# A four-layer fp32 transformer stack on one core: head-norm sums by token block on 128 partitions, inverse roots updated in PSUM, high and low scales spread by one product

## What is computed

```python
def rms_norm(x, g):
    xf = x.astype(jnp.float32)
    y = xf * lax.rsqrt(jnp.mean(xf * xf, axis=-1, keepdims=True) + EPS)
    return (y * g.astype(jnp.float32)).astype(x.dtype)

# in the attentions, per head:
q = rms_norm(q.reshape(B, S, HEADS, HEAD_DIM), q_gain)
k = rms_norm(k.reshape(B, S, KV_HEADS, HEAD_DIM), k_gain)
```

## Time and profile before

| | |
|---|---|
| median of 3 runs | 2533.02 us (2532.95 to 2538.74) |
| the profiled execution | 2532.64 us, of which the profile's span is 2530.8 us |
| mean granted TensorE clock | 0.972 of full |
| PE busy | 2378.3 us, 94% of the span |
| POOL busy | 1685.3 us, 67% |
| DVE busy | 1113.7 us, 44% |
| ACT busy | 495.5 us, 20% |
| HBM | 82 GB/s mean |

### The profile page before, as it was taken

How to read it: one execution, slowest core, us unless ns; L and a number is a source line. 1 busy time by engine, 2 the same in 40 slices (tenths; PEclk the granted TensorE clock), 3 DMA queues, 4 the chain that set the end, 5 groups by cost and what they waited for, 6 DMA issues and landing times.

```text
span 2530.8 us, 29132 instructions
## 1 busy us (share of the span) xinstructions
PE 2378.3 (94%) x10786; PEld 1915.5 (76%) x10786; DVE 1113.7 (44%) x1306; ACT 495.5 (20%) x926; POOL 1685.3 (67%) x1370
## 2 busy tenths in 40 slices
PE   5978999999997899999999799999999898999999
PEld 4766788888766678888887568888877675888887
DVE  7674543322367444332248645215344443550440
ACT  3245111110124511111011511001111163110000
POOL 5465677777746567777776668767775554776774
PEclk9988999999998899999999899999999999999999
DMA  4300122222320012222232122222222200222222
GB/s 143 113 17 17 61 89 99 99 83 93 114 98 24 17 67 85 98 99 85 92 122 100 39 79 83 100 100 100 98 102 84 84 17 17 95 95 96 97 100 83
DMA packets 37840, 207.88 MB, mean 82 GB/s; under 512 B 3532, under 2 KB 10316, under 8 KB 16888
## 3 DMA queue, kind: packets, MB, share of 16 engines
q1 hardware_dynamic: 37752, 206.70, 23.5%
HBM read 204.55 MB, written 2.13 MB: 82 GB/s over the span
## 4 chain that ended last, share of the span: by engine, by line
PE 59%; DVE 4%; POOL 2%; ACT 2%; issue 1%; DVEq 0%; POOLq 0%; ACTq 0%
PE ps L822 18%; PE ps L827 18%; PE ps L826 18%; POOL wl L650 1%; PE ps L1184 1%; PE ps L895 1%; PE ps L1158 1%; ACT rt L1334 1%; DVE nt L1702 0%; DVE t L1710 0%; DVE nt L1710 0%; POOL wh L644 0%; POOL act L722 0%; PE ps L1159 0%; PE ps L1160 0%
## 5 line engine op out<-in xcount | busy, mean ns | idle before, releaser
L650 POOL TENSOR_TENSOR wl<-raw,wh 128x512 fp32r<-128x512 f32 (+1 forms) x776 | 1049.3, 1384 | 0.0
L644 POOL TENSOR_SCALAR wh<-raw 128x1024 fp32r<-128x1024 f32 (+1 forms) x388 | 430.7, 1130 | 597.1 <-PE ps L822 469.9
L822 PE MATMUL ps<-h,wh 128*128 128x512 f32 x1576 | 617.3, 392 | 21.8 <-POOL wl L650 9.2
L827 PE MATMUL ps<-h,wl 128*128 128x512 f32 x1576 | 613.9, 390 | 0.0
L826 PE MATMUL ps<-h,wh 128*128 128x512 f32 x1576 | 613.8, 389 | 0.0
L822 PE MATMUL ps<-act,wh 128*128 128x512 f32 x1120 | 437.9, 391 | 3.1 <-POOL act L722 2.1
L826 PE MATMUL ps<-act,wh 128*128 128x512 f32 x1120 | 436.3, 390 | 0.0
L827 PE MATMUL ps<-act,wl 128*128 128x512 f32 x1120 | 436.2, 389 | 0.0
L822 PEld LDWEIGHTS ps<-h,wh 128*128 128x128 f32 x1576 | 296.2, 188 | 91.3 <-issue 26.3
L826 PEld LDWEIGHTS ps<-h,wh 128*128 128x128 f32 x1576 | 296.2, 188 | 62.0 <-issue 1.0
L827 PEld LDWEIGHTS ps<-h,wl 128*128 128x128 f32 x1576 | 296.1, 188 | 61.8
(11 more groups left out here) (339 smaller groups left out, 2824.9 us busy)
## 6 DMA issues: line engine op xcount, KB each, us to landing
raw<-w_gu SPq DMA_DIRECT2D x44, 1024.0 KB, 4.8
raw<-w_up SPq DMA_DIRECT2D x32, 1024.0 KB, 4.8
raw<-w_down_b SPq DMA_DIRECT2D x32, 1024.0 KB, 4.9
raw<-w_down_a SPq DMA_DIRECT2D x32, 704.0 KB, 4.0
raw<-w_in_a SPq DMA_DIRECT2D x14, 1024.0 KB, 4.9
raw<-w_in_f SPq DMA_DIRECT2D x13, 1024.0 KB, 4.9
raw<-w_in_r SPq DMA_DIRECT2D x11, 1024.0 KB, 4.9
raw<-w_out_a SPq DMA_DIRECT2D x8, 1024.0 KB, 7.7
```

Of the source, the lines that this page charges most:

```text
L644: pool.tensor_scalar(hi_s[:, part], raw[s][:, part], 1.0, 1.0, ALU.mult, ALU.mult).then_inc(hi_done, 1)
L650: ins = pool.tensor_tensor(lo_s[:, part], raw[s][:, part], hi_s[:, part].bitcast(F32), ALU.subtract)
L822: first = pe.matmul(out, w_hi, v_hi, start=start, stop=False)
L827: return pe.matmul(out, w_lo, v_hi, start=False, stop=stop)
```

## The change

1. `gathered`: the product over 512 (or 256) tokens becomes four of 128 (or 64) tokens each; block q goes to the partitions 32q to 32q+31 of the same bank. The sums of 16 groups by 512 tokens stand on 128 partitions by 128 columns instead of 32 by 512.
2. ACT's `stat` does one more instruction, Square of the first root, into `nt[:, 2]`. Head norms run on 128 x 128 (128 x 64).
3. DVE's Newton step keeps its running value in the PSUM bank: for head norms three instructions (scalar_tensor_tensor, tensor_scalar, tensor_tensor), for row norms four, each with at most one input in SBUF. The bank is handed back (`free[b]`) after the last of them instead of after the first.
4. `head_stat` then writes the high part (four tensor_scalar of 32 x 128 from PSUM) and the low part (four tensor_tensor of 32 x 128, PSUM minus the high part) into the two halves of 64 rows of one tile, `rs[place]`.
5. `spread_to`: one product on 64 rows instead of two on 32.

The core of the diff:

```diff
@@ gathered (PE)
-                pe.matmul(ps[b][0:32, 0:width], gather[rows, kind, w0:w0 + 32], sq[rows, n % 2, 0:width],
-                          start=start, stop=stop).then_inc(ready[b] if stop else sq_used, 1)
+                w = width // TB
+                for q in range(TB):
+                    last = pe.matmul(ps[b][32 * q:32 * q + 32, 0:w], gather[rows, kind, w0:w0 + 32],
+                                     sq[rows, n % 2, q * w:(q + 1) * w], start=start, stop=stop)
+                last.then_inc(ready[b] if stop else sq_used, 1)
@@ spread_to (PE)
-                rows = slice(group, group + 32)
-                pe.matmul(ps[b][:, 0:width], spread[rows, idx, :], rsh[rows, 0:width], start=True, stop=False)
-                pe.matmul(ps[b][:, 0:width], spread[rows, idx, :], rsl[rows, 0:width], start=False,
+                pe.matmul(ps[b][:, 0:width], spread[rows, idx, :], rs[place][rows, 0:width], start=True,
                           stop=True).then_inc(ready[b], 1)
@@ stat (ACT)
-                fn(nt[rows, 1, 0:n], nt[rows, 0, 0:n], ACT.Exp, scale=-0.5).then_inc(stat_y, 1)
+                fn(nt[rows, 1, 0:n], nt[rows, 0, 0:n], ACT.Exp, scale=-0.5).then_inc(act_step, 1)
+                sc.wait_ge(act_step, step.up())
+                fn(nt[rows, 2, 0:n], nt[rows, 1, 0:n], ACT.Square).then_inc(stat_y, 1)
...
-                stat(4, 0, slice(0, 32), T, 1.0)
+                stat(4, 0, full, P, 1.0)
@@ stat and head_stat (DVE)
-                v, y, w = nt[rows, 2, 0:n], nt[rows, 1, 0:n], nt[rows, 0, 0:n]
-                tsc(v, ps[b][rows, 0:n], scale, EPS, ALU.mult, ALU.add, bk.empties(b, u))
-                tt(w, y, y, ALU.mult)
-                stt(v, w, -0.5, v, ALU.mult, ALU.mult)
-                stt(out, v, 1.5, y, ALU.add, ALU.mult, sdone)
-
-            def head_stat(b, u, n, group):
-
-                stat(b, u, slice(0, 32), n, 1.0, t[0:32, 3, 0:n])
-                rows = slice(group, group + 32)
-                tsc(rsh[rows, 0:n], t[0:32, 3, 0:n], 1.0)
-
-                tsc(t[rows, 2, 0:n], t[0:32, 3, 0:n], 1.0)
-                tt(rsl[rows, 0:n], t[rows, 2, 0:n], rsh[rows, 0:n].bitcast(F32), ALU.subtract, rsr)
+                v = ps[b][rows, 0:n]
+                if scale == 1.0:
+                    stt(v, v, EPS, nt[rows, 2, 0:n], ALU.add, ALU.mult)
+                else:
+                    tsc(v, v, scale, EPS, ALU.mult, ALU.add)
+                    tt(v, v, nt[rows, 2, 0:n], ALU.mult)
+                tsc(v, v, -0.5, 1.5, ALU.mult, ALU.add)
+                return v
+
+            def stat(b, u, rows, n, scale, out):
+
+                v = inverse_root(b, u, rows, n, scale)
+                tt(out, v, nt[rows, 1, 0:n], ALU.mult, sdone)
+                dve.sem_inc(free[b], 1)
+
+            def head_stat(b, u, n, place, row=0):
+
+
+                w = n // TB
+                v = inverse_root(b, u, full, w, 1.0)
+                tt(v, v, nt[:, 1, 0:w], ALU.mult, sdone)
+                hi_rows, lo_rows = slice(row, row + 32), slice(row + 32, row + 64)
+                for q in range(TB):
+                    cols = slice(q * w, (q + 1) * w)
+                    tsc(rs[place][hi_rows, cols], ps[b][32 * q:32 * q + 32, 0:w], 1.0)
+                for q in range(TB):
+                    cols = slice(q * w, (q + 1) * w)
+                    tt(rs[place][lo_rows, cols], ps[b][32 * q:32 * q + 32, 0:w], rs[place][hi_rows, cols].bitcast(F32),
+                       ALU.subtract, chain if q < TB - 1 else rsr)
+                dve.sem_inc(free[b], 1)
```

More of the change, by code:

```diff
@@ L199, with __init__ @@
 class Mixer:
-    def __init__(self, kind, name, heads, per_unit, rows, scale, tile0, group, kidx):
+    def __init__(self, kind, name, heads, per_unit, rows, scale, tile0, place, kidx):
         self.kind, self.name, self.heads, self.per_unit = kind, name, heads, per_unit
-        self.rows, self.scale, self.tile0, self.group, self.kidx = rows, scale, tile0, group, kidx
+        self.rows, self.scale, self.tile0, self.place, self.kidx = rows, scale, tile0, place, kidx
         self.units = heads // per_unit
@@ L265 @@
 SWA = Mixer("band", "swa", 6, 2, 64, 1.0, 0, 0, None)
-MLA = Mixer("causal", "mla", 6, 1, 96, MLA_SCALE, 5, 32, 6)
+MLA = Mixer("causal", "mla", 6, 1, 96, MLA_SCALE, 5, 1, 6)
 FOX = Mixer("causal", "fox", 8, 2, 64, 1.0, 0, 0, 4)
-XA = Mixer("full", "xa", 4, 1, 128, XA_SCALE, 4, 32, 0)
+XA = Mixer("full", "xa", 4, 1, 128, XA_SCALE, 4, 1, 0)
 def build(nc, a):
@@ L317, in build @@
         spread = keep("spread", [N_SPREAD, P], F32R)
-        rsh = keep("rsh", [T], F32R)
-        rsl = keep("rsl", [T], F32R)
+        rs = [keep(f"rs{i}", [T], F32R) for i in range(2)]
         cs = keep("cs", [T])
@@ L1098, in start @@
                 if m.name == "mla":
-                    spread_to(7, 0, 9, m.group)
+                    spread_to(7, 0, 9, m.place)
                 prep(m, 0)
@@ L1452, in in_a @@
                     square(11 + i, slice(0, 96), ps[tt % 4][0:96, :])
-                stat(5, 0, slice(0, 32), T, 1.0)
+                stat(5, 0, full, P, 1.0)
                 bk.close(USES_IN_A)
@@ L1482, in in_r @@
                     square(4 + i, full, rxk[:, i, :], M_MEM)
-                stat(5, 0, slice(0, 32), M_MEM, 1.0)
+                stat(5, 0, full, M_MEM // TB, 1.0)
                 for i in range(4):
@@ L1530, in in_f @@
                     square(8 + i, full, fxq[:, i, :])
-                stat(4, 1, slice(0, 32), T, 1.0)
+                stat(4, 1, full, P, 1.0)
                 stat(7, 1, full, M_MEM, 1.0 / D)
@@ L1538, in in_f @@
                     square(12 + i, full, fxk[:, i, :], M_MEM)
-                stat(5, 1, slice(0, 32), M_MEM, 1.0)
+                stat(5, 1, full, M_MEM // TB, 1.0)
                 bk.close(USES_IN_F)
@@ L1933, in in_r @@
                 mem_out(t[:, 1, :])
-                head_stat(4, 0, T, 32)
+                head_stat(4, 0, T, 1)
                 mem_keys(12, rxk, t[:, 1, :])
-                head_stat(5, 0, M_MEM, 64)
+                head_stat(5, 0, M_MEM, 1, 64)
                 bk.close(EARLY_IN)
@@ L2001, in in_f @@
                     evac((17 + i) % 4, (17 + i) // 4, fxq[:, i, :])
[L2002 to L2005, removed]
+                head_stat(4, 1, T, 1)
                 mem_out(fe)
@@ L2011, in in_f @@
                     mem_values(25, fxv, i)
-                head_stat(5, 1, M_MEM, 64)
+                head_stat(5, 1, M_MEM, 1, 64)
                 bk.close(late(USES_IN_F))
@@ L2125, in attention @@
                 if m.name == "swa":
-                    head_stat(5, -1, T, 32)
+                    head_stat(5, -1, T, 1)
                 for hd in range(m.heads + 2):
@@ L2238, in constants @@
             c[lo:hi, C_GATHER + 64 * kind + 32 + k] = 1 / (hi - lo)
-    for group in (0, 32, 64):
+    for group in (0, 32, 64, 96):
         for i in range(N_SPREAD):
```

14 lines of the change are left out of this document (7 added, 7 removed).

## The result

The changed kernel takes **2480.46 us** (median of 4 runs, 2478.7 to 2482.26) against 2532.98 (4 runs) of the kernel before on the same chip: a ratio of 0.9787 with a 95% interval of 0.9776 to 0.9799, 52.5 us less. Forecast were 24.4. The profiled execution took 2481.47 us, its span is 2479.7, 51.1 shorter than before; the mean granted clock is 0.974. Where such a difference is read from one execution of each kernel, it is good to some 2.5 us.

What follows compares the result with a forecast made beforehand. PE bounds the kernel, busy 2378 of 2531 us, with POOL the next limit. Terms 5.0 + 3.7 + 2.4 + 6.2 + 8.6 - 1.5 = 24.4 us off 2532.64 gave a median of 2508.5, range 2489 to 2521.

Steps and rivals of the forecast that it cites:

- the gathers: PE, 42 of 52 gathers counted: four pieces of 128 columns cost 0.03 us more than one product; -1.5 us.
- Rival 1: Gathers: column groups overlap, 0.54 instead of 0.86 us; 2499, or 2494 if ACT does not hold; chance 0.3.
- (a): SWA, two layers: a shorter head norm cuts PE's waits of 1.62 and 1.93; 2.5 us each, in all 5.0.
- (d): `in_f` before FOX, once: PE's 6.55 wait for bank 6 shrinks, next chunk at 1990.3 instead of 1996.6; 6.2 us.
- (c): Start of `in_f`, once: PE's 2.44 wait behind the first evacuations and both row norms goes; 2.4 us.
- (b): `in_r`, once: PE's 3.67 wait for the squares of the memory keys goes in full; 3.7 us.
- The spreads: PE, 58 calls of `spread_to`: the removed product saves 0.23 us at 512 columns; three quarters of 11.5 taken, 8.6.
- Rivals 2 and 3: Rival 2: column changes dear, 2555, chance 0.08; rival 3: gains do not reach the end, 2517 or 2525, chance 0.12.

Runs made afterwards that it cites:

- the ladder: Change added stepwise to the kernel before: single spread 2522.2, direct high and low 2513.6, Newton step in PSUM 2500.3, gathers by token block 2480.5 us.
- the ladder's second step: Direct writes of high and low parts from PSUM, added to the kernel before with the single spread: 2513.6 us.
- wide gathers: Changed kernel with part 1 alone undone, each gather again one product of 32 partitions by 512 (256) columns: 2500.3 us.

## Why the prediction was wrong

**The term that failed: the gathers.** The prediction took four pieces of 128 columns to stream "as much" as one of 512, 0.88 for 0.86, from the fp32 products of the earlier trace rows, and booked 1.5 us of loss. Those rows are full-width products, of which each needs all columns of the array. They bound a product that has the array to itself, not four that have a quarter each: kept on one group, the pieces did cost 1.06 us, and on four 0.43. (Nor does the 1.5 follow from its own working: 42 gathers at 0.03 are 1.3.) Measured: a gain of 19.8 us. The difference, 21.3, is three quarters of the 28.1 us by which the forecast missed.

**Rival 1 named the mechanism and sized it too small.** It had the pieces overlap, but made the second pass of each piece wait for its own first and hold the pieces behind, 0.54 a gather. The records show no such hold: four in a row take 0.25 each with the squares ready. It also let ACT's squares leave only 0.16 for gathers in a row. They do hold PE, yet four take 2.1 instead of 3.7 us, so 0.4 each is left. With the measured prices the rival's own sum becomes 10 x 0.61 for those alone, 24 x 0.4 for those of 512 columns in a row and 8 x 0.17 for those of 256 (four take 2.24 us wide and 1.54 in pieces), 17.1 in all. That is what the trace shows at the gathers; 19.8 were measured, and no run places the rest. So the rival's counts of 10 and 32 fit, and its saving on a lone gather and on one of 512 columns in a row, 0.32 and 0.16, was half or less of the true one. The Trainium skill, TensorE: Matmul & The Clock Gate, Part 3, gives 2.38 for three column tiles; here four gave 1.06 / 0.43 = 2.5 for a lone gather and 0.92 / 0.25 = 3.7 in a row. As an estimate, that factor on the 0.86 of a lone gather saves 0.50, so rival 1's 0.32 was not this rule's, as the prediction had it; 0.61 were measured. The prediction had this rule in hand and let the absence of a row speak against it.

**DVE's terms (a) to (d): 17.3 forecast, 22 measured** as the two middle steps of the ladder. The lengths were right (3.5 for 3.6 us; 0.30 and 0.70 a row; the gap before FOX 1.79, "under 1.8"). By the trace (c) brought 2.8 for 2.4, (d) 5.7 for 6.2, (b) 5.6 for 3.7, its cheaper gathers included, and (a) 4.4 in each layer for 2.5, its spreads included. The gaps of (a) shrank by what it said, 1.62 + 1.93 - 1.10 = 2.45 us in the first layer. What it left out is the clock. Windows in the kernel before, from the 1.93 us gap on, and in the changed one over the same products (PE's granted clock is the third column from the end):

```profile
152.00:154.00 2.00, 1.15 (x5) 1.15 (x6) 1.82 (x3) 1.45 (x5) 1.26 (x1) 0.67 0.00 0
154.00:156.00 2.00, 2.00 (x11) 2.00 (x10) 0.17 (x1) 0.20 (x2) 0.00 (x0) 0.50 0.00 0
156.00:158.00 2.00, 2.00 (x15) 1.87 (x15) 0.00 (x0) 1.07 (x3) 0.00 (x0) 0.98 0.00 0
```
```profile
146.00:148.00 2.00, 1.60 (x13) 1.61 (x14) 1.90 (x4) 0.34 (x2) 1.82 (x2) 1.00 0.00 0
148.00:150.00 2.00, 2.00 (x16) 1.88 (x15) 1.19 (x2) 1.52 (x4) 0.41 (x1) 1.00 0.03 8
```

After the two gaps PE ran at half its clock, 1.2 GHz, up to 156; with one gap of 1.10 the granted clock stays full, 2.4 GHz. The 18 products of 256 columns that follow take 3.68 us before (152.85 to 156.53) and 2.24 after (146.40 to 148.64). The traces of the other runs bear this out. At the same place, in both layers A:

| profiles | first gap (1.62), us | second gap (1.93), us | the 18 products, us |
|---|---|---|---|
| before, before with gathers twice, single spread alone | 0.98 to 1.88 | 1.93 to 2.17 | 3.06 to 4.00, in 6 of 6 |
| the other 13, whose head norm takes 5.8 us or less | none | 0.78 to 1.89 | 2.24 to 2.26, in 26 of 26 |

The longest second gap that left the clock full, in the second layer of the repeated run with row norms in SBUF (timeline, then the window over it):

```profile
766.06 0.39 PE L1159 MATMUL ps<-qh,khb_swa 128*128 128x256 f32 x1 [1.89 <-ACT dg_swa L1335]
766.00:768.00 2.00, 1.94 (x16) 1.94 (x17) 1.56 (x4) 0.92 (x4) 0.71 (x1) 1.00 0.00 0
```

So a shorter head norm takes the half clock away here, worth 1.4 us in the first layer and 0.8 in the second (3.06 to 2.25) beyond the gaps. It comes with the ladder's second step, which takes out the first gap; whether by that or by the length of the second, the runs don't tell. It is no rule for one gap: behind the 1.79 us before FOX the changed kernel ran at half clock up to 1951, and behind 1.80 in its second run at full. The prediction priced the gaps of (a) at their own length and not at what followed; in (d) it did read the spreads at half clock.

The clock moves once more, in MLA of the first layer; before, and then after over the corresponding products:

```profile
204.00:208.00 4.00, 4.00 (x10) 2.76 (x11) 1.79 (x3) 0.69 (x2) 1.42 (x2) 0.50 0.00 0
208.00:212.00 4.00, 3.89 (x20) 3.63 (x19) 0.42 (x1) 2.17 (x6) 0.00 (x0) 0.66 0.00 0
```
```profile
196.00:200.00 4.00, 4.00 (x10) 2.96 (x11) 1.85 (x3) 1.29 (x3) 1.50 (x2) 0.50 0.02 4
200.00:204.00 4.00, 3.23 (x23) 2.75 (x22) 1.44 (x4) 2.77 (x7) 0.73 (x1) 1.00 0.00 0
```

By windows of 1 us the full clock is back at 210.7 before and already at 200.0 after, nine products sooner in the list, and in the kernel before it falls again from 214.1 to 217.5. Over the same products, up to 217.28 and 205.99, that stretch takes 11.44 us before and 8.92 after, 2.5 less. This is not (a)'s: the kernel with the single spread alone has its two gaps in SWA and takes 9.18 here, while the kernel before with gathers twice takes 11.45. It came with part 5, though issuing every spread twice in the changed kernel does not bring it back (9.40), so its cause stays open.

**The spreads: 8.6 and 0.5 forecast, 9.2 by doubling, 8.7 to 10.8 by the ladder.** Right in size; that a part of the ladder's figure is the clock in MLA was not in the forecast.

**Rivals 2 and 3.** Going from one column group to the next costs nothing that shows: a second set of pieces over all four groups costs 0.13 us a gather. A later release ends none of PE's gaps over 0.45 us except the one before FOX, where 1.79 was foreseen. The count of instructions went up and the time down.

## What to carry to other kernels

A product that uses 32 of the array's 128 weight columns can be cut into four by its moving side, one on each column group: eight records took 0.43 us instead of 1.06, and the sums land on all 128 partitions, which also cuts the rows that the other engines read. Bound such a term from a row that really shares the resource; where none exists, keep the full concurrency as an end of the range. Where GpSimd and DVE contend, keep a chain's running value in PSUM, so that each instruction has at most one input in SBUF: it is the inputs that count, since rows that write PSUM from SBUF alone (`ps<-nt`) still took up to 1.67 us. And price a PE gap together with the clock that follows it.

## What the runs showed of the hardware

- Four fp32 products of 128 x 128 on four column groups, two passes each, cost 0.25 us together where they follow others of their kind (kernel with four square buffers), and 0.92 as one product of 512 columns on one group (wide gathers).
- DVE instructions that write PSUM and read it, with at most one input in SBUF, take the time of those that only read it: in the changed kernel 0.28 to 0.30 at 128 columns, 0.70 at 512 (all 36) and 0.17 at 2. With all inputs in SBUF 128 columns took 0.29, 1.00 and 0.30 in one chain, 512 took 1.29, 0.68 and 1.64; the last of these wrote PSUM.
- One kernel's time moves with the mean granted clock of the execution: the kernel before took 2527.4 to 2534.9 us where the mean was 0.970 to 0.972, and 2536.8 to 2538.9 where it was 0.967 or 0.968.
- Two such gathers of 64-column pieces took 0.25 us in a row (timeline of the kernel with four square buffers, PE, layer R), so the time still follows the columns at that size:

```profile
1354.01 0.43 PE L900 MATMUL ps<-sq,gather 128*32 128x64 f32 x16
1354.26 0.29 PE L900 MATMUL ps<-t,gather 128*32 128x64 f32 x8
```
